# Layer 1's conditioning sums: four column strips of one PSUM bank in place of one strip over two banks

## The reference

```python
def ada_params(cvec, w, b):
    return jnp.split(jax.nn.silu(cvec) @ w + b, 6, axis=-1)

for l in range(DEPTH):
    need_ctx = l < DEPTH - 1
    sh1, sc1, g1, sh2, sc2, g2 = [m[:, None, :] for m in ada_params(c, ada_w[l], ada_b[l])]
    csh1, csc1, cg1, csh2, csc2, cg2 = ada_params(c_ctx, ada_w[l], ada_b[l])
    h = pre_mod(x, mix_pre_g[l], sh1, sc1)          # rms_norm * (1 + scale) + shift
    ...
    x = post_add(x, y, mix_post_g[l], g1)           # x + gate * rms_norm(y)
    f = conv_ffn(pre_mod(x, ffn_pre_g[l], sh2, sc2), ffn_w_up[l], ffn_conv_w[l], ffn_conv_b[l], ffn_w_down[l])
    x = post_add(x, f, ffn_post_g[l], g2)
```

## Time and profile before

| | us |
|---|---|
| median of three runs | 1597.65 |
| the profiled execution | 1596.83 |
| its span | 1595.0 |
| TensorE busy | 1487.5 (93%) |
| VectorE busy | 966.3 (61%) |
| ScalarE busy | 722.4 (45%) |
| GpSimd busy | 596.5 (37%) |
| up0: window 371 to 725 | 354.0, TensorE busy 352.96 |
| down0: window 725 to 890 | 165.0, TensorE busy 164.74 |

### The profile page before, as it was taken

The page is one execution under the profiler, slowest core; times in us unless marked ns, Lnnn a source line. Parts: engine busy times, 40 slices in busy tenths (PEclk is TensorE's granted clock), DMA queues, the critical chain, the costliest instruction groups (busy, mean ns, idle before and its releaser), DMA issues.

```text
span 1595.0 us, 22240 instructions
## 1 busy us (share of the span) xinstructions
PE 1487.5 (93%) x7628; PEld 1202.1 (75%) x7628; DVE 966.3 (61%) x1476; ACT 722.4 (45%) x1242; POOL 596.5 (37%) x529
## 2 busy tenths in 40 slices
PE   4988898999999999999999698899999999999997
PEld 1877467787888888887888576677777888888886
DVE  2457687557687668743334575788885544444455
ACT  2332476544332333223353545487775544444453
POOL 2351354242222222322333531375552344443454
PEclk8999899999999999999999899999999999999999
DMA  8230850112464346311222111110002233332232
GB/s 336 56 98 1 293 184 1 53 59 87 145 184 117 109 145 184 105 40 53 63 65 66 48 53 55 52 53 1 1 1 81 78 93 94 103 92 67 92 95 103
DMA packets 128122, 143.89 MB, mean 90 GB/s; under 512 B 7164, under 2 KB 95488, under 8 KB 127024
## 3 DMA queue, kind: packets, MB, share of 16 engines
q1 hardware_dynamic: 128048, 142.91, 28.6%
HBM read 140.79 MB, written 2.10 MB: 90 GB/s over the span
## 4 chain that ended last, share of the span: by engine, by line
PE 82%; DVE 7%; ACT 3%; DMA 3%; POOL 2%; issue 2%; SPq 0%; DVEq 0%; POOLq 0%; ACTq 0%
PE ps L470 23%; PE ps L471 22%; PE ps L472 22%; PE ps L1427 4%; PE ps L1413 3%; PE ps L1438 2%; DMA start_w<-in_ada_w_dram 2%; PE ps L1440 2%; DMA ada_w<-in_ada_w_dram 1%; PE ps L2075 1%; PE ps L1330 1%; POOL w_lo L462 1%; PE ps L924 1%; DVE hT_lo L803 1%; ACT prob L1467 1%
## 5 line engine op out<-in xcount | busy, mean ns | idle before, releaser
L462 POOL TENSOR_TENSOR w_lo<-raw,w_hi 128x1024 fp32r<-128x1024 f32 (+1 forms) x183 | 346.9, 1898 | 627.5 <-ACT w_hi L455 627.5
L470 PE MATMUL ps<-hT_hi,w_hi 128*128 128x512 f32 (+1 forms) x1096 | 387.5, 354 | 9.3 <-DVE hT_lo L803 5.0
L471 PE MATMUL ps<-hT_lo,w_hi 128*128 128x512 f32 (+1 forms) x1096 | 384.8, 351 | 0.0
L472 PE MATMUL ps<-hT_hi,w_lo 128*128 128x512 f32 (+1 forms) x1096 | 382.6, 349 | 0.0
L455 ACT ACTIVATE w_hi<-raw 128x1024 fp32r<-128x1024 f32 (+1 forms) x200 | 172.9, 866 | 197.0 <-PE ps L472 166.2
L470 PEld LDWEIGHTS ps<-hT_hi,w_hi 128*128 128x128 f32 x1096 | 207.1, 189 | 47.1 <-DVE hT_lo L803 6.0
L472 PEld LDWEIGHTS ps<-hT_hi,w_lo 128*128 128x128 f32 x1096 | 206.5, 188 | 28.8
L471 PEld LDWEIGHTS ps<-hT_lo,w_hi 128*128 128x128 f32 x1096 | 207.1, 189 | 26.9
L2301 DVE TENSOR_TENSOR g_lo<-act_g,g_hi 128x768 fp32r<-128x768 f32 (+1 forms) x82 | 104.2, 1277 | 155.9 <-ACT g_hi L2256 155.5
L470 PE MATMUL ps<-w_hi,g_hi 128*128 128x512 f32 x410 | 160.4, 391 | 3.5 <-DVE g_lo L2301 3.0
L472 PE MATMUL ps<-w_hi,g_lo 128*128 128x512 f32 x410 | 159.6, 389 | 0.0
(11 more groups left out here) (247 smaller groups left out, 2500.7 us busy)
## 6 DMA issues: line engine op xcount, KB each, us to landing
raw<-in_ffn_w_up_dram SPq DMA_DIRECT2D x84, 512.0 KB, 3.9
ada_w_up<-in_ada_w_dram SPq DMA_DIRECT2D x48, 512.0 KB, 4.2
raw<-in_ffn_w_down_dram SPq DMA_DIRECT2D x84, 256.0 KB, 2.6
ada_w<-in_ada_w_dram SPq DMA_DIRECT2D x32, 512.0 KB, 5.2
start_w<-in_ada_w_dram SPq DMA_DIRECT2D x8, 1024.0 KB, 11.4
raw<-in_c_w_qkv_dram SPq DMA_DIRECT2D x12, 512.0 KB, 3.7
raw<-in_ab_w_in_dram SPq DMA_DIRECT2D x8, 512.0 KB, 4.8
raw<-in_ab_w_out_dram SPq DMA_DIRECT2D x8, 512.0 KB, 4.3
```

The lines of the kernel that those rows point to most:

```text
L462: by.tensor_tensor(w_lo[:, slot, 0:width], raw[:, n % RAW, 0:width], w_hi[:, slot, 0:width].bitcast(F32), ALU.subtract).then_inc(lo_split, 1)
L470: nc.tensor.matmul(outp, s_hi, m_hi, start=first, stop=False, skip_group_check=True)
L471: nc.tensor.matmul(outp, s_hi, m_lo, start=False, stop=False, skip_group_check=True)
L472: return nc.tensor.matmul(outp, s_lo, m_hi, start=False, stop=last, skip_group_check=True)
```

## The change

The sums of layer 1's conditioning go to four strips of 32 partitions of bank 6: partition 64v + 32·half + (5 - i) holds block i of stream v, columns of that half. Bank 7 isn't used for them any more. A matmul of the sums writes strip r = 64v + 32·half; the number of these matmuls stays 16, their order too. The clearing matmuls become four, one for each strip. Both streams share one selector, so VectorE copies one per turn and not two. At the end of up0 VectorE copies the whole bank (128 by 512) into the accumulator's memory in place of 32 by 1024 into `gate_rows`. In down0 the small loads become 16 of half rows in place of 8, the bias sum four instructions of 6 by 512 in place of one of 12 by 1024, the transposes four in place of eight, the column steps twelve instructions of four columns in place of eight of eight columns (the second shift and scale of the context, which nothing reads, are left out), and the multiplication by the gains two of 6 by 512. Layer 1's gates read the same number of columns from other rows.

```diff
         def ada_row(l, i, v):
-            return 96 + 2 * (5 - i) + v if l else 2 * i + v if i < 2 else 32 + 2 * (i - 2) + v
+            return 64 * v + 5 - i if l else 32 + 2 * (i - 2) + v
...
+        def ada1_small_loads(sp):
+            for v in range(2):
+                for i in range(6):
+                    r = ada_row(1, i, v)
+                    sp.dma_start(beside_up[2][r:r + 33:32, 0:BANK],
+                                 ada_b[1, i * D:(i + 1) * D].rearrange("(h n) -> h n", n=BANK)
+                                 ).then_inc(s("ada_rows_landed"), 16)
+            for g, r in ((ffn_post_g, 0), (mix_post_g, 3)):
+                for half in range(2):
+                    sp.dma_start(beside_up[3][32 * half + r:32 * half + r + 3, 0:BANK],
+                                 g[1, half * BANK:(half + 1) * BANK].partition_broadcast(3)
+                                 ).then_inc(s("ada_rows_landed"), 16)
...
-        def ada_turn(pe, n, b):
+        def ada_rows_turn(pe, n, b):
             pe.wait_ge(s("ada_biased"), n)
-            for k in range(KC):
-                mm = nc.tensor.transpose(bank(b, 2 * BANK)[:, k * P:(k + 1) * P], gate_rows[:, k * P:(k + 1) * P],
-                                         ident[:, :])
+            for c in range(4):
+                mm = nc.tensor.transpose(bank(b)[:, c * P:(c + 1) * P], gate_rows[:, c * P:(c + 1) * P], ident[:, :])
             mm.then_inc(s("ada_turned"), 1)
...
+        def ada1_bias(dve):
+            dve.wait_ge(s("ada_rows_landed"), 16 * (2 + ADA1_SMALL))
+            for v in range(2):
+                for half in range(2):
+                    rows = slice(64 * v + 32 * half, 64 * v + 32 * half + 6)
+                    op = nc.vector.tensor_tensor(gate_rows[rows, 0:BANK], ada1_rows[rows, :], beside_up[2][rows, 0:BANK],
+                                                 ALU.add)
+            op.then_inc(s("ada_biased"), 1)
...
+        def ada1_columns(dve):
+            dve.wait_ge(s("ada_turned"), 2)
+            turned = bank(6).rearrange("p (c r) -> p r c", r=P)
+            for sub, v in ((0, 0), (0, 1), (1, 0)):
+                for half in range(2):
+                    kk = slice(4 * half, 4 * half + 4)
+                    r = 32 * half + ada_row(1, 3 * sub, v)
+                    g = 16 * sub + 8 + 4 * half
+                    nc.vector.tensor_copy(add_col[:, sub, v, kk], turned[:, r, :])
+                    nc.vector.scalar_tensor_tensor(out=mul_col[:, sub, v, kk], in0=turned[:, r - 1, :], scalar=1.0,
+                                                   in1=cols[:, g:g + 4], op0=ALU.add, op1=ALU.mult)
+            for half in range(2):
+                rows = slice(32 * half, 32 * half + 6)
+                nc.vector.tensor_tensor(gate_rows[rows, 0:BANK], gate_rows[rows, 0:BANK], beside_up[3][rows, 0:BANK],
+                                        ALU.mult)
...
             if l == 0:
-                for half in range(2):
-                    nc.tensor.matmul(ps[96:128, 6 + half, :], select[:, 0:32],
+                for r in range(0, P, 32):
+                    nc.tensor.matmul(ps[r:r + 32, 6, :], select[:, 0:32],
...
             def ada_sums(i, ada_streams):
                 pe.wait_ge(s("ada_mac"), i * (2 * KC) + START_MACS)
-                pe.wait_ge(s("ada_selector"), i * 2)
+                pe.wait_ge(s("ada_selector"), i)
                 for v in range(ada_streams):
                     for half in range(2):
-                        mm = nc.tensor.matmul(ps[96:128, 6 + half, :], select_v[:, v, :],
+                        r = 64 * v + 32 * half
+                        mm = nc.tensor.matmul(ps[r:r + 32, 6, :], select_v[:, :],
                                               beside_up[0][:, v, half * BANK:(half + 1) * BANK],
                                               start=False, stop=True, skip_group_check=True)
...
-                        nc.vector.tensor_copy(gate_rows[96:128, :], psf[96:128, 6 * BANK:8 * BANK])
+                        nc.vector.tensor_copy(ada1_rows, bank(6))
...
-                        for v in range(2):
-                            nc.vector.tensor_copy(select_v[:, v, :], select[:, bass.ds(i * 2 + (22 - v), 32)]
-                                                  ).then_inc(s("ada_selector"), 1)
+                        nc.vector.tensor_copy(select_v[:, :], select[:, bass.ds(i + 27, 32)]).then_inc(s("ada_selector"), 1)
```

More of the change, by code:

```diff
@@ L233, in hybrid_backbone_kernel @@
         select = keep("select", [P, 64])
-        select_v = keep("select_v", [P, 2, 32])
+        select_v = keep("select_v", [P, 32])
         fold = keep("fold", [P, 2, 32])
@@ L265, in hybrid_backbone_kernel @@
                                conv_at, conv_at + KB4)
+        ada1_rows = beside_up[0][:, 0, 0:BANK]
         tops = [tail, xn_at + 12 * KB4, conv_at + 3 * 4 * TOK + 2 * KB4]
@@ L574, in ada_load @@
             sp.dma_start(mem[1][n % ADA_RING][:, :], ada_w[l, rows, cols_]).then_inc(s(f"ada_landed{n % ADA_RING}"), 16)
[L576 to L585, removed]
+        ADA1_SMALL = 16
+        def ada1_small_loads(sp):
[9 more added lines that the diff above has]
+                                 g[1, half * BANK:(half + 1) * BANK].partition_broadcast(3)
                                  ).then_inc(s("ada_rows_landed"), 16)
@@ L700, in start_tensor @@
                         norm_turn(pe, "mix0", k)
[L701 to L704, removed]
-            mm.then_inc(s("ada_turned"), 1)
+            ada_rows_turn(pe, 1, START_TURNED)
             close(pe, "pe")
@@ L1604, in gate_tensor @@
                 v, half = divmod(i, 2)
-                row = ada_row(l, (2, 5)[sub], v)
+                row = ada_row(l, (2, 5)[sub], v) + 32 * l * half
+                c0 = 0 if l else half * BANK
                 if i >= 2:
                     pe.wait_ge(s(f"{tag}_gate"), i - 1)
-                nc.tensor.matmul(bank(6 + i % 2), ident[:, row:row + 1].broadcast_to([P, P]),
-                                 gate_rows[:, half * BANK:(half + 1) * BANK],
+                nc.tensor.matmul(bank(6 + i % 2), ident[:, row:row + 1].broadcast_to([P, P]), gate_rows[:, c0:c0 + BANK],
                                  start=True, stop=True, skip_group_check=True).then_inc(s(f"{tag}_gate_mm"), 1)
@@ L2187, in down_sync @@
                     after_phase(sp, 6)
-                    ada_small_loads(sp, beside_up, 1, range(6))
+                    ada1_small_loads(sp)
                 with sp.Fori(0, DTURNS) as i:
@@ L2222, in down_tensor @@
                     pe.wait_ge(s(f"{tag}_gate"), 4)
-                    ada_turn(pe, 2, 6)
+                    ada_rows_turn(pe, 2, 6)
                 with pe.Fori(1, DTURNS - 1) as i:
@@ L2314, in down_vector @@
                 dve.wait_ge(s("ffnpost0_gate_mm"), 4)
-                ada_bias(dve, beside_up, 2, 10, 96, 12, gate_rows[96:108, :])
+                ada1_bias(dve)
             split_activations(1, 0, DTURNS // 2)
             if l == 0:
-                ada_columns(dve, 2, 1, range(6), 6)
-                ada_gates(dve, beside_up, 2, 96, 12)
+                ada1_columns(dve)
             first_half_vector(dve, f"ffnpost{l}", nt, lambda t: four(y0d[:, t, :]))
```

## The result

The changed kernel took 1587.35 us (median of 7 runs, 1582.49 to 1589.10), beside 1597.47 for the kernel before in 7 runs (1595.70 to 1603.56). The ratio is 0.993, with a 95% interval of 0.9910 to 0.9949 (8.1 to 14.4 us), 10.1 us by the medians. A second comparison (8 runs beside 13 of the kernel before) gave 0.994 (0.9921 to 0.9960). The profiled execution took 1587.08 us, 9.75 less than the profiled one of before, with a span of 1585.3. The forecast was 1587.9, and 1587.1 on the profiled execution's base.

The account below looks back on a forecast made before the run. TensorE was taken to bound the kernel; 5.10 (groups of four), 3.40 (groups of two), 0.83 (clearing) and 0.43 (transposes) make 9.76 us less, 1587.9 from the median of 1597.65, range 1585.8 to 1591.6.

Parts of the forecast that it names:

- The sum: TensorE in up0 and down0: groups of four 5.10, groups of two 3.40, clearing 0.83, transposes 0.43; 9.76 us less.
- 0.98 for two strips: Up0, four groups of two sums: each falls from 1.83 to 0.98 us, 3.40 us less; bounds 0.97 and 1.83.
- The edits priced at nothing: Edits on VectorE and SyncE and layer 1's gates: their added time fits in slack, so no cost to the kernel.
- The bias sum: VectorE in down0: four instructions take 2.4 to 2.7 us, 1.2 to 1.5 more; nothing, with 5.5 us in reserve.
- the sixteen issues: SyncE in down0: small loads at 0.29 us each put the weight load back some 1.4 us, over 6 early; nothing.
- The twelve column steps: VectorE in down0: 1.0 to 1.4 us in place of 0.68; with the gains 0.3 to 0.9 more, within 1.4 slack.
- the gains: VectorE in down0, the multiplication by the gains: 1.2 to 1.4 us in place of 1.22, costing nothing.
- A: Rival, up0: only groups of four overlap, pairs go one behind the other; 6.4 us won, 1591.3; chance 7%.
- B: Rival, up0: passes run in strict program order, four strips 2.26 us, two 1.40; 4.3 us won, 1593.4; chance 5%.
- The estimate from the same page of the Trainium skill: Up0 sums: 3.2 times for four strips, 1.6 for two, 1.12 and 1.16 us a group; about 8.7 us less.
- C: Rival, down0: VectorE's added steps make g_lo 2.3 us later, 0.9 past its slack; 1588.8; within the forecast's 84%.
- D: Rival, down0: sixteen small loads land late, bias sum delays g_lo, TensorE waits at half 1; slower, 1604 if at 825; 3%.

Follow-up runs that it names:

- e5: The changed kernel with every sum made twice, the strips in the order 0, 32, 64, 96, 0, 32, 64, 96; 1596.67 us, middle stretch 5.18 us longer.
- e6: The changed kernel with every sum made twice, each followed at once by its own repetition (0, 0, 32, 32, ...); 1592.03 us, middle stretch 5.25 us longer.
- e8: The changed kernel with 32 small loads in place of 16 in down0, all waited for by the bias sum; 1590.05 us, middle stretch 0.06 us longer.
- e11: The changed kernel with 48 small loads in place of 16 in down0; 1599.56 us in one execution, middle stretch 9.84 us longer.
- e7: The changed kernel with 36 more four-column copies on VectorE in front of the gains in down0; middle stretch 1.28 us longer, no whole time given.

## Why the prediction was right

**The bound.** TensorE waits for no other engine in the middle stretch but in the wait of 1.62 us at its end, which both kernels have. Every microsecond that left its queue there left the end.

**The sum.** The forecast was 9.76 less, and 9.76 were measured. The one value without a row, 0.98 for two strips, came out as 0.98; its bound of 1.83 would have made 1591.3. Taking it next to the row of line 1330 was right because a group's cost is that of its fullest strip (0.43 us for a record of 512 columns) plus 0.11 to 0.16, whatever the number of strips; e5 and e6 show the same with two layers.

**The base.** The forecast of 1587.9 used the median of three runs; the seven of the comparison had a median of 1597.47. That the changed kernel's own profile read 1587.08, forecast as 1587.1 on that base, is luck in part: -1.36 and +1.4 us elsewhere cancelled.

**The edits priced at nothing.** They cost nothing, but two of their sizes were off. The bias sum took 3.89 us and not 2.4 to 2.7, and the sixteen issues 7.6 and not 4.7. Both were held by slack that the prediction had read (5.5 us at half 1, over 6 at the weight load); the load was at last 2.5 us early (it went out at 790.54, lands in 2.6 and is read at 795.63). The twelve column steps took 0.83 us, under the 1.0 to 1.4 forecast, and the gains 1.36, within theirs; together they added 0.3.

The slack behind them was read wrong. The prediction halved the 2.91 us of two `g_lo` and had the first end at 851.2, 1.4 us early. A window around it shows that one alone:

```profile
849.71 2.04 DVE L2301 TENSOR_TENSOR g_lo<-act_g,g_hi 128x768 fp32r<-128x768 f32 x1
```

It lasts 2.04 us beside a `w_lo` of GpSimd and ends at 851.75, 0.8 us before ScalarE's 852.57. The upper end of what the prediction added, 0.9, would have been 0.1 too much: the rows it had read didn't show that the whole addition fits. In the changed kernel the first `g_lo` ends at 840.83 for a `w_hi` at 841.45, 0.6 us early: a second gate step is held up (5.80 us for the six against 4.80 before), and this `g_lo` isn't (0.95). So the price of nothing was right, but on less slack than stated, and that the steps added only 0.3 is luck in part.

**The rivals.** A falls by the pairs of 0.98. B falls by the groups of 1.00 and 0.98, for its 2.26 and 1.40, and by e6. The sentence of the Trainium skill (TensorE: Matmul & The Clock Gate, section "The mechanism") that matmuls are strictly ordered in their starts doesn't hold for this form: e6's records disagree with it. The estimate from the same page of the Trainium skill (section "Measured speedup vs the span model", 2.38 times for three column tiles) would have made 8.7 us; the trace shows 3.6 times for four strips. C named the place rightly; it overpriced the steps, which went at 0.07 us each, and took the slack there for 1.4 us where it was 0.8. D's wait comes only between twice and three times the loads, and then by the weight load behind them rather than by the bias sum (e8, e11).

## What to carry to other kernels

Small fp32 matmuls with 32 output columns cost by the fullest strip of 32 partitions of the output, so spread them over all four, cutting the moving columns if there are too few matmuls (1.83 to 0.98 to 0.57 us for the same sum here). Their order in the program doesn't matter, nor does the bank. To judge a gain under 1% read it between two fixed places of the bounding engine: it repeated to 0.01 us, while whole executions differed by 6.6 (7 of the changed kernel) and by 11.8 (13 of the kernel before). And where a row gives several instructions together, read them one by one: half of two was 0.6 us off.

## What the hardware showed that was not expected

- **VectorE instructions that come to an end only behind GpSimd's.** The selector copy of turn 1 in the changed kernel, and GpSimd beside it:

```profile
434.55 1.23 DVE L2169 COPY select_v<-select 128x32 f32 x1
```

```profile
433.32 2.42 POOL L463 TENSOR_TENSOR w_lo<-raw,w_hi 128x1024 fp32r<-128x1024 f32 x1 [7.26 <-ACT w_hi L456]
```

  The copy of 32 columns ends at 435.78 and GpSimd's instruction at 435.74. In turn 0 the copy begins 0.25 us before GpSimd's ends (385.68) and takes 0.29, so it ends 0.04 behind it too. Longer instructions end later by nearly their usual length. A gate step and the `w_lo` beside it:

```profile
838.18 1.78 DVE L1671 TENSOR_TENSOR y0d<-y0d,gate 128x512 f32<-128x512 f32 x1
```

```profile
838.08 1.33 POOL L463 TENSOR_TENSOR w_lo<-raw,w_hi 128x512 fp32r<-128x512 f32 x1 [2.77 <-ACT w_hi L456]
```

  It ends at 839.96, 0.55 us behind GpSimd's 839.41, and the other steps of that form last 0.68. Three of the four bias sums took 0.67 to 0.68 us and the fourth 1.82, to 0.56 us behind a `w_lo`; in e8 and e11, where GpSimd began none before the last of the four was under way, all four took 2.77 together. The `g_lo` of 2.04 us in the kernel before ends 0.82 us behind its `w_lo`, and one beside none takes 0.95. So a held instruction seems to do its work when GpSimd's is over. The hold also goes the other way: where a gate step had begun first, a `w_lo` lasted 1.60 us (e7, 840.30) and 1.73 (kernel before, 849.20) in place of 1.30. The second taps (L2155, which read PSUM) ran from 433.50 to 434.63 beside the same GpSimd instruction in their usual 1.13 us for two. Which operand forms are held up wasn't tried.
- **A small load's issue costs by its form.** 0.25 us for two neighbouring rows of 4 KB in the kernel before, 0.47 to 0.55 for two rows of 2 KB that lie 32 partitions apart, and 0.26 to 0.43 for three rows of 2 KB from one source row.
